# Recurrent rounds of a hybrid RWKV-7 and attention trunk: all of TensorE's flips and projection chunks as 64x64 quarters

## The reference

```python
def step(state, inp):
    r_t, w_t, k_t, v_t, a_t, b_t = inp
    sa = jnp.einsum('bhij,bhj->bhi', state, a_t)
    state = (state * w_t[:, :, None, :] + sa[..., None] * b_t[:, :, None, :]
             + v_t[..., None] * k_t[:, :, None, :])
    return state, jnp.einsum('bhij,bhj->bhi', state, r_t)
```

## Time and profile before

| | us |
|---|---|
| median of three runs | 1778.16 (1777.97 to 1778.27) |
| profiled execution | 1777.27 |
| its span, first to last instruction | 1775.5 |
| the rounds k = -1 to 8, in it | about 109 to 465 |
| one round (k = 3) | 40.6 |

### The profile page before, as it was taken

One profiled execution on the slowest core, in us unless ns is written; L12 is line 12 of the kernel. 1 busy time (PEld: TensorE's weight loads), 2 busy tenths in 40 slices (PEclk: granted clock), 3 DMA queues, 4 the chain that ended last, 5 costly groups with the idle time before them and its releaser, 6 DMA issues.

```text
span 1775.5 us, 35844 instructions
## 1 busy us (share of the span) xinstructions
PE 1742.2 (98%) x15388; PEld 1351.5 (76%) x15388; DVE 904.0 (51%) x1567; ACT 742.5 (42%) x1285; POOL 202.0 (11%) x172
## 2 busy tenths in 40 slices
PE   7999999999999999999999999999999999999999
PEld 2746666666478888888888888888887788888887
DVE  6825555554454444333556656655656544444321
ACT  6434444432243222222565665565655532222211
POOL 0033344431100000000111111111110000000000
PEclk9999999999999999999999999999999999999999
DMA  4321222231133223333322222322222233333332
GB/s 128 99 64 61 88 68 68 66 104 62 60 96 95 95 95 96 106 95 95 104 81 89 84 83 73 85 82 83 84 84 72 72 95 95 95 98 101 98 95 95
DMA packets 58453, 155.00 MB, mean 87 GB/s; under 512 B 6503, under 2 KB 23447, under 8 KB 58296
## 3 DMA queue, kind: packets, MB, share of 16 engines
q1 hardware_dynamic: 58200, 152.63, 27.7%
q10 hardware_dynamic: 96, 0.07, 0.0%
HBM read 150.51 MB, written 11.61 MB: 91 GB/s over the span
## 4 chain that ended last, share of the span: by engine, by line
PE 92%; DVE 4%; ACT 2%; issue 1%; DMA 1%; POOL 1%; SPq 0%; ACTq 0%; DVEq 0%; POOLq 0%
PE bank L618 89%; PE bank L621 2%; DVE f L2278 1%; DVE f L2193 0%; DVE r L2107 0%; ACT f L1684 0%; ACT r L1369 0%; DMA f<-xT 0%; ACT f L1686 0%; DMA f<-stream 0%; DMA f<-const 0%; DVE r L1785 0%; DVE f L1796 0%; DVE f L1809 0%; DVE f L1837 0%
## 5 line engine op out<-in xcount | busy, mean ns | idle before, releaser
L618 PE MATMUL bank<-r 128*128 128x512 f32 x5424 | 1253.4, 391 | 2.4 <-DVE r L2107 1.0
L618 PEld LDWEIGHTS bank<-r 128*128 128x128 f32 x5424 | 1012.6, 188 | 221.2 <-issue 6.2
L618 PE MATMUL bank<-f 64*64 64x64 f32 (+6 forms) x9532 | 457.1, 279 | 24.8 <-issue 5.2
L1785 DVE TENSOR_TENSOR r<-f,r 128x1024 fp32r<-128x1024 f32 x222 | 283.9, 1279 | 362.6 <-ACT r L1369 362.3
L618 PEld LDWEIGHTS bank<-f 64*64 64x64 f32 (+3 forms) x9532 | 291.3, 138 | 183.7 <-issue 112.3
L1369 ACT ACTIVATE r<-f 128x1024 fp32r<-128x1024 f32 x222 | 232.4, 1048 | 146.3 <-PE bank L618 141.5
L2465 POOL TENSOR_TENSOR r<-f,r 128x512 fp32r<-128x512 f32 x48 | 66.9, 1394 | 807.6 <-ACT r L1673 807.6
L1652 ACT ACTIVATE r<-f 128x512 fp32r<-128x512 f32 x44 | 27.8, 632 | 215.6 <-DVE f L2146 215.6
L2176 DVE TENSOR_TENSOR f<-bank,f 128x512 f32<-128x512 f32 x72 | 56.1, 778 | 74.9 <-PE bank L618 72.2
L1684 ACT ACTIVATE f<-bank,f 128x512 f32<-128x512 f32 x48 | 33.0, 688 | 101.5 <-PE bank L618 100.8
L1649 ACT ACTIVATE f<-f 128x512 f32<-128x512 f32 x44 | 27.8, 632 | 110.5 <-DVE f L2136 110.5
(11 more groups left out here) (117 smaller groups left out, 926.2 us busy)
## 6 DMA issues: line engine op xcount, KB each, us to landing
f<-stream SPq DMA_DIRECT2D x246, 512.0 KB, 3.6
bias_copies<-bias_rows SPq DMA_DIRECT2D x6, 1536.0 KB
f<-xT SPq DMA_DIRECT2D x16, 256.0 KB, 4.4
f<-lora_out SPq DMA_DIRECT2D x16, 128.0 KB, 6.2
f<-bias_copies SPq DMA_DIRECT2D x64, 32.0 KB, 2.4
f<-bias_copies SPq DMA_DIRECT2D x32, 64.0 KB, 2.1
outT<-f SPq DMA_DIRECT2D x8, 256.0 KB, 4.5
f<-const SPq DMA_DIRECT2D x1, 576.0 KB, 3.7
```

What stands on the lines that cost most here:

```text
L618: return nc.tensor.matmul(out, lhsT, rhs, start=start, stop=stop, skip_group_check=True)
L1785: TT(r(lo_at(q), 1024), f(O_RAW + panel_of(q) % RAW * 1024, 1024), rf(hi_at(q), 1024), ALU.subtract).then_inc(s["w_lo"], 1)
```

## The change

- The three transposing flips and the value flip become products of 64x64 pieces (`flip_corners`): 16 for each flip, with the piece as weight and the identity's (or the centring matrix's) diagonal piece as the moving side. A head's two pieces go to side bank 0 or 1, by head, so each flip now fills 256 columns in both banks, and ScalarE reads both with one copy. For that the two banks are one tensor, `sides`.
- The removal and b flips come one behind the other into the two halves of the side banks, with one signal at the end.
- The uses of the side banks are set in a new order: all flips count as uses of bank 0, and wait for bank 1's last reader beside it. The variance sum moves to bank 7, with a semaphore of its own (`var_ln`) that later writers of bank 7 wait for.
- All 16 steps of rounds 0 to 7 are in quarters.
- On VectorE the addition of the value's far half comes before the fifth masking.

```diff
-        QUARTERED = (0, 3, 4, 6, 7, 9, 10, 11, 12, 13, 14, 15)
         def quartered(k, step):
-            return 0 <= k < NHP and step in QUARTERED
+            return 0 <= k < NHP
...
-        SIDE = {0: [("b_tr", 0), ("akv", 0), ("bonus", 1), ("var", -1),
+        SIDE = {0: [("v_tr", 0), ("b_tr", 0), ("akv", 0), ("k_tr", 0), ("bonus", 1),
                     ("first", 1), ("bsc", 1), ("ksc", 1), ("w", 2), ("g", -1)],
-                1: [("kk", 1), ("v_tr", 0), ("a_tr", 0), ("k_tr", 0), ("first", 1), ("bsc", 1), ("ksc", 1),
-                    ("a", 2)]}
+                1: [("kk", 1), ("first", 1), ("bsc", 1), ("ksc", 1), ("a", 2)]}
...
             def variance_ready(hp):
-                fill(0, "var", hp)
+                pe.wait_ge(s["y_sb"], hp + 1)
                 pe.wait_ge(s["y_sq"], hp + 1)
...
+            def flip_corners(at, off, by):
+
+                for q in range(NT):
+                    for e in range(2):
+                        for h in range(2):
+                            last = mm(banks[h][CH * e:CH * (e + 1), at + q * HD:at + (q + 1) * HD],
+                                      half(off(q) + e * CH, h), half(O_CON + by + h * HD, h))
+                return last
+
             def value_flip(hp):
-                fill(1, "v_tr", hp)
+                fill(0, "v_tr", hp)
+                if hp + 1 < NHP:
+                    side_read(pe, 1, "kk", hp + 1)
+                else:
+                    side_read(pe, 1, "ksc", hp)
                 if hp:
                     projection_kept(pe, proj_of_value(hp))
-                for q in range(NT):
-                    last = mm(banks[1][:, q * P:(q + 1) * P], f(vin(hp) + q * P, P), con(C_CENTRE))
-                last.then_inc(s["v_tr"], 1)
-
-            def removal_flip(hp):
-                fill(1, "a_tr", hp)
+                flip_corners(0, lambda q: vin(hp) + q * P, C_CENTRE).then_inc(s["v_tr"], 1)
+
+            def removal_and_b_flip(hp):
+                fill(0, "b_tr", hp)
                 pe.wait_ge(s["ar_a"], hp + 1)
-                for q in range(NT):
-                    last = flip(banks[1][:, q * P:(q + 1) * P], f(chunk(O_AR, hp, 2 * P, q, 0), P))
-                last.then_inc(s["a_tr"], 1)
-
-            def b_flip(hp):
-                fill(0, "b_tr", hp)
+                flip_corners(0, lambda q: chunk(O_AR, hp, 2 * P, q, 0), C_ID)
                 pe.wait_ge(s["bt"], hp + 1)
-                for q in range(NT):
-                    last = flip(banks[0][:, q * P:(q + 1) * P], f(chunk(O_BT, hp, P, q, 0), P))
-                last.then_inc(s["b_tr"], 1)
+                flip_corners(4 * HD, lambda q: chunk(O_BT, hp, P, q, 0), C_ID).then_inc(s["b_tr"], 1)
...
             def first_inverse(hp):
...
+                if hp:
+                    side_read(pe, 0, "k_tr", hp - 1)
...
-                    off_diagonal(k, 5, (lambda q, h: sum_beside(0, O_Y, "var_ps", q, h)) if before else None)
+                    off_diagonal(k, 5, (lambda q, h: sum_beside(7, O_Y, "var_ps", q, h)) if before else None)
...
+            def flipped(at):
+
+                return sides[:, :].rearrange("p (h q n) -> p h q n", h=2, n=HD)[:, :, at * NT:(at + 1) * NT, :]
...
             def keep_removal(hp):
-                side(1, (s["a_tr"], hp + 1), bc(f(O_YY, 2 * S), (S, 2), (P, NT), (1, HD)),
-                     in_=banks[1][:, :].rearrange("p (q h n) -> p h q n", q=NT, h=2), scale=-1.0)
+                act.wait_ge(s["b_tr"], hp + 1)
+                A(bc(f(O_YY, 2 * S), (S, 2), (P, NT), (1, HD)), flipped(0), ACT.Copy, scale=-1.0)
...
                 if here:
+                    add_far(proj_of_value(k + 2), vin(k + 2))
                     x_masked(k, 5)
-                    add_far(proj_of_value(k + 2), vin(k + 2))
                     keep_inverse(k, 5)
```

More of the change, by code:

```diff
@@ L254, in trunk @@
         ctx.enter_context(nc.sbuf_tensor("whole_map", [P, TOTAL], F32))
-        banks = [ctx.enter_context(nc.psum_tensor(f"bank{i}", [P, 512], F32)) for i in range(8)]
+        sides = ctx.enter_context(nc.psum_tensor("sides", [P, 1024], F32))
+        banks = [sides[:, 0:512], sides[:, 512:1024]]
+        banks += [ctx.enter_context(nc.psum_tensor(f"bank{i}", [P, 512], F32)) for i in range(2, 8)]
         bias_rows = nc.dram_tensor("bias_rows", [3 * 16 * 384], F32, kind="Internal").ap()
@@ L849, in k_flip @@
             def k_flip(hp):
-                fill(1, "k_tr", hp)
+                fill(0, "k_tr", hp)
                 pe.wait_ge(s["kt"], hp + 1)
-                for q in range(NT):
-                    last = flip(banks[1][:, q * P:(q + 1) * P], f(chunk(O_KT, hp, P, q, 0), P))
-                last.then_inc(s["k_tr"], 1)
+                flip_corners(0, lambda q: chunk(O_KT, hp, P, q, 0), C_ID).then_inc(s["k_tr"], 1)
             def first_inverse(hp):
@@ L1502, in decays_back, with tokens @@
                 A(f(O_EM), f(O_CC), ACT.Exp, scale=KAPPA).then_inc(s["em"], 1)
+            def flipped(at):
+                return sides[:, :].rearrange("p (h q n) -> p h q n", h=2, n=HD)[:, :, at * NT:(at + 1) * NT, :]
+            def tokens(off):
+                return bc(f(off), (HD, 2), (P, NT), (1, HD))
             def keep_value(hp):
-                side(1, (s["v_tr"], hp + 1), f(O_VTOK))
+                side(0, (s["v_tr"], hp + 1), tokens(O_VTOK), in_=flipped(0))
             def keep_removal(hp):
-                side(1, (s["a_tr"], hp + 1), bc(f(O_YY, 2 * S), (S, 2), (P, NT), (1, HD)),
-                     in_=banks[1][:, :].rearrange("p (q h n) -> p h q n", q=NT, h=2), scale=-1.0)
+                act.wait_ge(s["b_tr"], hp + 1)
+                A(bc(f(O_YY, 2 * S), (S, 2), (P, NT), (1, HD)), flipped(0), ACT.Copy, scale=-1.0)
             def keep_b(hp):
-                side(0, (s["b_tr"], hp + 1), f(O_BTOK))
+                side(0, (s["b_tr"], hp + 1), tokens(O_BTOK), in_=flipped(1))
             def keep_k(hp):
-                side(1, (s["k_tr"], hp + 1), f(O_KTOK))
+                side(0, (s["k_tr"], hp + 1), tokens(O_KTOK), in_=flipped(0))
             def keep_a_k_v(hp):
@@ L1559, in deviation @@
                     act.wait_ge(s["fin"], hp)
-                side(0, (s["var_ps"], hp + 1), f(O_RS), ACT.Ln, bias=kol(K_LNEPS), scale=1.0 / HD)
-                side_read(act, 0, "var", hp)
+                act.wait_ge(s["var_ps"], hp + 1)
+                A(f(O_RS), banks[7][:, :], ACT.Ln, bias=kol(K_LNEPS), scale=1.0 / HD).then_inc(s["var_ln"], 1)
+                act.wait_ge(s["var_ln"], hp + 1)
                 A(f(O_RS), f(O_RS), ACT.Exp, scale=-0.5).then_inc(s["y_rs"], 1)
```

11 lines of the change are left out of this document (6 added, 5 removed).

## The result

The changed kernel takes **1801.64 us** in the median (1799.24 to 1802.65, four runs) against 1778.22 for the kernel before in the same comparison; the ratio is 1.0127, interval 1.0109 to 1.0144. The forecast was 1768.7 with a range to 1773.8: wrong in sign. What was forecast as the unlikeliest rival (TensorE outruns its instructions) is what happened, larger than I had made it.

The account below looks back on a forecast made before the run. TensorE's instructions were taken to bound every round. Gains of 10.8 us over eight rounds, less 1.3 for instruction stops, took 9.5 off the profiled 1777.3, giving 1767.8; that execution lay 0.9 under the median, so 1768.7, range 1765.8 to 1773.8.

Parts of the forecast that it names:

- TensorE outruns its instructions: Rival: from value flip to k flip, two instruction stops of 0.9 us each round, 14.4 against 10.8; 1781.8 us, chance 0.03.
- The visit: Each switch of TensorE to whole-array work and back costs 0.33 us; four of five go in a round, gaining 1.32.
- the value flip: In each round, 8 whole-array passes of 0.87 us become 8 sets of quarter passes of 0.46, gaining 0.41.
- the transposes: Removal, b and k flips: 12 transposes of 1.31 us a round become 24 sets of 1.39, losing 0.08.
- chunks in quarters: Chunks 1, 2, 5 and 8 as four products of 64x512 take the same time, beside the visit: nothing gained.
- Chunk 8: It waits for the moved far addition, so 0.26 of its visit's 0.33 us is lost and 0.07 kept.
- What no longer hides what: Flips sharing bank 0, fewer signals and the variance sum in bank 7 were to bring no wait that costs time.
- The supply of instructions: TensorE's stops for late instructions in the rounds were to grow by between 0 and 4.8 us; 1.3 was taken.
- the moved addition: Rival: with a late near-half copy, chunk 8 and inverse step 5 come up to 0.6 later; 1771.0 us, chance 0.07.
- four passes: Rival: flip products replacing transposes need four passes, not two, giving back 1.39 us a round; 1778.5 us, chance 0.03.
- the cheaper visit: Rival: a switch to the whole array costs half of 0.33 us, 5.3 less gain; 1774.0 us, chance 0.06.
- The signs of being wrong: A flip of 0.9 us, fifth masking over 0.2 after off-diagonal 5, or "issue" stops over 7 us in the rounds.

Follow-up runs that it names:

- runs 1: The kernel before, each product of a quarter chunk split into two of 256 columns, 96 passes more a round; 1791.23 us, ratio 1.0053.
- 8: The changed kernel with its flips as 8 products of 128 columns, half of each flip's tokens left out, 64 passes fewer a round; 1786.59 us, ratio 1.0044.
- runs 9: The kernel before with value flip, k flip and chunks 1 and 5 in quarters, bias copies in their old place; 1781.45 us, ratio 1.0000.
- 10: The kernel before with only the removal and b flips and chunk 2 in quarters, bias copies in their old place; 1787.04 us, ratio 1.0030.
- run 4: The changed kernel with the six bias copies moved from rounds 0 to 5 into the first feed-forward; 1787.82 us, ratio 1.0035.
- 6: The kernel before with value flip and chunk 1 in quarters and the bias copies moved out of the rounds; 1777.77 us, ratio 0.9992.
- 3: The kernel before with only the value flip and chunk 1 in quarters, bias copies in their old place; 1787.05 us, ratio 1.0031.
- 7: The kernel before with value flip, k flip and chunks 1 and 5 in quarters, bias copies moved out of the rounds; 1771.16 us, ratio 0.9954.
- the split one: The kernel before with each quarter-chunk product split into two of 256 columns; 1791.23 us, or 1787.85 with the bias copies out of the rounds.
- run 2: The changed kernel with chunk 8 whole again and the far addition back behind the fifth masking; 1797.57 us, ratio 1.0089.

## Why the prediction was wrong

- *What bounds the kernel.* TensorE, wholly, in each round: right for before. But in its densest stretches before was already close to a second bound, TensorE's supply of instructions.
- *The visit, 1.32 us a round, and the value flip, 0.41; the transposes, 0.08 lost; chunks in quarters, nothing.* The flips were right. The visits were priced too low: the three beside chunk 8's and the flips gave 1.64 in clean stages (1.52 against the usual round) for 1.32 in the forecast, so 0.40 to 0.44 for a visit instead of 0.33.
- *Chunk 8, 0.07 kept of its visit.* Wrong in sign: 0.18 lost. Off-diagonal 5 ended sooner than I had it and the start behind the addition took 0.15.
- *What no longer hides what.* Right. No new wait on bank 0 or for a copy of a flip shows in the rounds; the bonus sum, the flips and the variance sum brought none. The wait before off-diagonal 4 of round 6, which was to grow by 0.3, isn't there any more.
- *The supply of instructions, 1.3 us in all.* **This step failed**: stops went from 5.2 to 32.6 us, and small gaps and the waits that follow late products add to that. I had scaled the stops by the number of passes in a round (12% more) and allowed one more stop of 0.6 a round at most. In its place runs 1 and 8 show that passes alone make stops, runs 9 and 10 that the same count can cost 0 or 5.6 us, so that the count isn't all, and run 4 against the changed kernel, 6 against 3 and 7 against 9 that the bias copies raise the price. The rows to read were there. Before's own packets start at least 3.42 us apart, with some 127 passes for each; the change puts 128 passes into 1.86 us. The packets' mean interval in the rounds, which I gave as about 4 us (321.4 / 67 = 4.8), tells nothing of such a stretch.
- *The rivals.* "Slower: TensorE outruns its instructions" named the place and the mechanism, from value flip to k flip, and the point from which it decides (1.35 us of new stops a round; measured (32.6 - 5.2) / 8 = 3.4). Its chance of 0.03 was what was wrong, and the stop size: up to 2.8 us, not 0.9. I let myself be led by the fact that stops cost before only 5 us. The other rivals didn't come. Their times stand on two footings: those of the moved addition and of four passes leave out the 1.3 of stops (with them 1772.3 and 1779.8), that of the cheaper visit has them in.
- *The signs of being wrong.* Two of the three came: stops of over 7 us, and the fifth masking, which in round 3 starts 0.25 us after the end of off-diagonal 5 (285.61 against 285.36) where 0.2 was the limit. The third, a flip of 0.9 us, did not.
- *Two rules weighed.* The Trainium skill ("Runtime: NRT & Kernel Launch", Instruction fetch mechanics) holds that refills in 16 KiB blocks are mostly hidden. Here they are not: 37 of some 74 packets in the rounds went with a stop. Its rule on transpose mode ("TensorE: Matmul & The Clock Gate", Terms) did not decide: a flip made of products took 0.46 us, where the transposes had taken 0.44.

The sum, put right: 8 x 1.46 = 11.7 us gained (10.7 by the usual round), 27.4 of stops without a wait lost, and some 9 or 10 more that I can't split. It is what is missing to the 25.3 that were measured, and no sum of its own. Known parts of it are TensorE's waits for other engines, 4.1 us before and 5.6 after in the view of waits, and at most 1.7 for the halved clock; the gaps under 0.2 us are not in the count of stops.

What stays open: by what way the bias copies hold instruction packets up; whether the density of a stretch or the place where packets end decides over a stop; why the copies matter in the changed kernel (14 us) and hardly in the split one (3 us); and how far the supply catches up in one whole chunk.

## What to carry to other kernels

Price an edit to TensorE's stream in instructions too: many small products in place of a few large ones cost nothing on the array and can still stop it. Look at the densest stretch, not at the average alone, and set its passes a microsecond against the smallest interval between instruction packets. Large whole-array products between dense stretches cut the stops here, but by no more than their switch cost. If such a kernel has stops, try first to start large DMA copies elsewhere: with that, and only the value and k flips in quarters, this kernel takes 1771.2 us, 0.46% less than before (0.16% by the moved copies alone).

## What the runs showed of the hardware

- In all sixteen traces of this study the packets of TensorE's instruction queue (16,384 bytes, about 127 float32 passes with their weight loads) start at least 3.2 us apart; in the changed kernel 36 of 37 stops end 2.2 to 3.7 us after a packet's start.
- Stops of 1.9 to 3.1 us were followed by 3.4 us at half the granted clock in eight cases, in six traces; a set of four 64x64 passes then went every 0.11 us instead of 0.058. Others as long, among them one of 3.1 us in run 2, were not.
- A change between whole-array and quarter products costs about 0.33 us for the way in and out by the starts in the kernel before, and 0.40 to 0.44 by what went when three of them went.
- In the first 45 us the granted clock differs between executions (0.78 over the first 20 us of the changed kernel's profile, 1.00 in that of before); its round 0 started at 132.8 against 132.7, so that didn't touch the comparison.
